# A hybrid attention, convolution, Fourier and expert kernel: the first expert tile's tokens picked by matmuls, weights ahead of casts, attention and preparation cut in units

## The chip, the cores and the metric
The kernel runs on the 8 cores of one Trainium2 chip. Each core computes one item of the batch, and no core talks to another. The metric is the device time of the slowest core in microseconds. Each core has TensorE (PE, matrix multiplication into the 8 banks of PSUM), VectorE (DVE), ScalarE (ACT), GpSimd (POOL) and SyncE (SP). POOL and SP issue the DMAs of this kernel. Each engine executes its instructions in order; semaphores join them.

## The reference
Two layers over 2048 latent tokens and 256 context tokens of width 1024, eight batch items. Cut to what matters:

```
cols = adaln(x) @ w_in                       # 1440 columns for three groups of heads
q = rmsnorm(rmsnorm(cq) @ w_uq); k, v = (rmsnorm(ckv) @ w_ukv), rotary part of k shared
attn = softmax(q k / sqrt(96)) v             # 8 heads, 2048 (+256) queries, 2304 keys
conv = silu(layernorm(depthwise_conv31(a * sigmoid(g))))
four = real(fft2(u)) over positions and channels of a group
x = x + gate * (concat(attn, conv, four) @ w_out)
layer 0: x = x + gate * swiglu(adaln(x))     # inner width 2816
layer 1: x = x + gate * sum over the top 2 of 8 experts of w_e * swiglu_e(adaln(x))
```

Modulation (`ada_w`) gives shift, scale and gate from a vector per batch item. The context goes the same way in layer 0; in layer 1 only its keys and values are used. Weights arrive as fp32; the matmuls are done in bf16. The output is the latent stream.

## The kernel before
**Residual stream.** `xT` (latent) and `cT` (context) hold the stream transposed, fp32, in SBUF for the whole program, as 4 blocks of 512 tokens and one of 256. A line such as `P.mm` records an instruction; the order of the recording is the order on each engine, and waits are derived from what each instruction reads and writes. So everything below has the order in which it is written. Helpers: `mm` L242, `transpose` L247, `act` L269, `tt` L273, `ts` L282, `stt` L296, `copy` L303, `recip` L307, `dma` L321, `gather` L329, `scatter` L336.

**Start.** 18 tiles of x and ctx are read and transposed by PE, with two buffers `xin`. `adab` (ada_w of layer 0, 8 pieces) is allocated in the memory which `xin` had, then `w_in` is loaded (L886).

**Projection.** For each block `adaln_steps` (L501) squares `xT` on ACT, sums over channels by a matmul with ones (`sq,cb`), and writes `hb`; `proj_units` gives 13 units of `w_in` matmuls. The steps for the next block are spread between the units of this one, and end with its last unit.

**Convolution, Fourier.** The convolution is 31 matmuls with diagonal matrices `dg` per 128 channels and block; its layer norm follows each block at once. `ada_rest` loads and multiplies one more piece of ada_w (`adab`) after each block. The Fourier part is matmuls with DFT matrices (`AB`). `out_proj(mixcf)` adds their share of the output projection to `xT` with `stt`.

**Attention.** `prep_steps(h)` makes `qf`, `kf`, `va` and the key scale `rk` of a head. Head 0's are done before attention, the next head's one step for each fourth attention step (`tick`). An attention step is one score matmul (128 keys, 512 queries), an `Exp` on ACT into `pt` and, two steps later (`LA`), the PV matmul. Scores have three PSUM banks. At the end of a query block `recip` and `tt` divide by the sum, from PSUM. `out_proj(mixa)` follows.

**Casts.** The expert weights are read as fp32 and written as bf16 to DRAM (`wsc`, `wsl`) by 48 casts (`mk_cast`, L838) of three DMAs each, on POOL's queue. A cast is an expert and a sixth of its inner width: three matrices, 3.15 MB written, the last sixth half of that. They wait for nothing. One stands before each layer's convolution, 18 lie in each layer's attention, 3 in layer 1's projection; the others are in the FFN and ahead of the experts. `w_outa`, `wr` (FFN weights) and `adab` load through the same queue.

**FFN of layer 0.** Six groups of inner columns (`mk_ffn`), with weights in two buffers `wr`; the first is loaded ahead of `out_proj(mixa)`. SP's queue zeroes the slot buffer `hs` from `zt` (23 DMAs) in that stretch.

**Experts of layer 1** (`moe_layer`, L548). The router transposes `xT` by tiles into token rows, writes x to the output, makes `hrow` (normed rows) and the logits. Slots come from sums by matmul. The 5888 slots are 23 tiles of 256 rows, each tile of one expert. 32 `scatter`s put each row into `hs` at both its slots. Each tile has six chunks of weights `wb[c]`, fetched by `gather` on POOL for the tile's expert; a gather reads `w_all` and so waits for all casts. `prep_h` loads a tile's rows (`hld`), and transposes them by matmuls (`cb,hld`) into `hTt`; `gu` and `down` are the expert matmuls, and a scatter-add puts the result in the output.

## Time and profile before

| | us |
|---|---|
| median of 3 runs | 4246.35 (4244.84 to 4509.96) |
| the profiled execution, device time | 4243.74 |
| its span on the slowest core (core 1) | 4242.7 |
| spans of the 8 cores | 4229.6 to 4242.7 |

| engine | busy us | share | instructions |
|---|---|---|---|
| TensorE matmuls | 3530.8 | 83% | 20731 |
| VectorE | 1568.6 | 37% | 2660 |
| ScalarE | 1579.4 | 37% | 3014 |
| GpSimd | 413.6 | 10% | 442 |

The span runs from the first to the last instruction. A busy share is a mean over stages which have different limits, so a stage must be read by its own rows. The granted clock of TensorE is told as a share of its full 2.4 GHz; its mean is 0.90. The DMA share is the mean busy share of the core's 16 DMA engines. The mean rate of DMA is 99 GB/s over 421.91 MB written; a cast counts with the bytes that it writes.

### The profile page before, as it was taken

What the parts mean: (1) busy time and instruction counts of PE and PEld (TensorE: products, weight loads), DVE (VectorE), ACT (ScalarE), POOL (GpSimd) and SP (SyncE); (2) the same over time, 40 slices, a digit from 0 to 9 for tenths busy, and PEclk for the clock granted to TensorE, in tenths of its full rate; (3) what the DMA queues carried; (4) which work ended last, traced back from release to release, by engine and by line L of the source; (5) the groups of instructions that cost most, each with busy time, mean ns of one, the idle gap of its engine ahead of it and who ended that gap; (6) DMA issues with size and microseconds to landing.
All of it is one profiled execution on the core that took longest, in us unless ns stands there. A gap on an engine that the chain in (4) does not pass through costs nothing.

```text
span 4242.7 us, 60869 instructions; the slowest of 8 cores (4229.6 to 4242.7 us)
## 1 busy us (share of the span) xinstructions
PE 3530.8 (83%) x20731; PEld 1917.3 (45%) x20731; DVE 1568.6 (37%) x2660; ACT 1579.4 (37%) x3014; POOL 413.6 (10%) x442
## 2 busy tenths in 40 slices
PE   4667777777879999767777878838999999999998
PEld 3224322222224555322322222316777777777776
DVE  1333545444544444433444444551222222222222
ACT  2433267777551111243267778321111111111111
POOL 0000201100000000000101010021111111111111
PEclk5778888888989999877888889869999999999999
DMA  7115499992494962633399997161555345425111
GB/s 166 30 26 90 55 108 111 112 106 39 101 162 59 121 93 43 81 38 40 58 108 102 108 102 92 75 228 52 179 200 191 93 131 192 161 56 189 31 26 21
DMA packets 215899, 421.91 MB, mean 99 GB/s; under 512 B 31952, under 2 KB 152272, under 8 KB 207312
## 3 DMA queue, kind: packets, MB, share of 16 engines
q0 software_dynamic: 186432, 347.15, 50.2%
q1 hardware_dynamic: 29168, 70.85, 5.2%
q8 instruction: 177, 2.90, 0.3%
q14 instruction: 122, 1.00, 0.1%
HBM read 833.76 MB, written 192.73 MB: 242 GB/s over the span
## 4 chain that ended last, share of the span: by engine, by line
PE 68%; DVE 10%; ACT 9%; issue 8%; DMA 3%; DVEq 0%; POOL 0%; ACTq 0%; another core or an unknown queue 0%; SPq 0%; POOLq 0%
PE psall L242 68%; DVE rec L307 3%; ACT pt L269 3%; DVE t L296 2%; ACT sqq L269 1%; DVE tmp L296 1%; DMA w_in<-w_in 1%; ACT L269 1%; DMA adab<-ada_w 1%; ACT rs L269 1%; DMA xin<-x 1%; ACT sq L269 1%; PE psall L247 1%; DVE xT L296 1%; DVE kf L282 1%
## 5 line engine op out<-in xcount | busy, mean ns | idle before, releaser
L242 PE MATMUL psall<-hTt,wb 128*128 128x256 bf16 x8096 | 908.5, 273 | 9.0 <-ACT hTt L269 8.6
L242 PEld LDWEIGHTS psall<-hTt,wb 128*128 128x128 bf16 x8096 | 791.5, 98 | 129.3 <-issue 12.7
L269 ACT ACTIVATE pt<-psall,rk 128x512 bf16<-128x512 f32 x1168 | 697.5, 720 | 62.8 <-PE psall L242 58.6
L242 PE MATMUL psall<-pt,va 128*128 128x512 bf16 x1168 | 490.1, 420 | 234.7 <-ACT pt L269 189.0
L273 DVE TENSOR_TENSOR aT<-sg,psall 128x256 bf16<-128x256 f32 x506 | 213.1, 421 | 1020.0 <-PE psall L242 993.1
L269 ACT ACTIVATE sg<-psall 128x256 f32<-128x256 f32 (+1 forms) x524 | 203.9, 390 | 1016.2 <-PE psall L242 1004.4
L242 PE MATMUL psall<-qf,kf 96*128 96x512 bf16 x1168 | 491.7, 422 | 0.0
L242 PE MATMUL psall<-wb,aT 128*128 128x512 bf16 x2024 | 459.2, 379 | 0.0
L242 PEld LDWEIGHTS psall<-pt,va 128*128 128x128 bf16 x1168 | 122.9, 105 | 602.2 <-issue 574.6
L242 PE MATMUL psall<-hT,wr 128*128 128x512 bf16 (+1 forms) x1760 | 354.7, 361 | 11.1 <-ACT hT L269 10.7
L307 DVE RECIPROCAL rec<-psall 64x512 f32<-64x512 f32 (+1 forms) x72 | 228.8, 3177 | 195.7 <-PE psall L242 194.6
L242 PE MATMUL psall<-hb,w_in 128*128 128x512 bf16 (+3 forms) x888 | 245.9, 434 | 58.9 <-ACT hb L269 46.1
L242 PEld LDWEIGHTS psall<-wb,aT 128*128 128x128 bf16 x2024 | 198.0, 98 | 209.6
L242 PEld LDWEIGHTS psall<-hT,wr 128*128 128x128 bf16 x1760 | 172.2, 98 | 185.0 <-issue 21.2
L296 DVE SCALAR_TENSOR_TENSOR xT<-psall,mod,xT 128x512 f32<-128x512 f32 x320 | 235.6, 749 | 46.5 <-PE psall L242 21.2
L269 ACT ACTIVATE sgt<-psall 128x512 f32<-128x512 f32 (+1 forms) x110 | 60.9, 553 | 432.1 <-PE psall L242 421.9
L329 POOL DMA_INDIRECT wb<-wsc,wix x115 | 115.8, 1007 | 931.7 <-PE psall L242 930.3
L242 PE MATMUL psall<-aT,wr 128*128 128x512 bf16 (+1 forms) x880 | 187.3, 365 | 21.1 <-DVE xT L296 19.0
L242 PEld LDWEIGHTS psall<-hb,w_in 128*128 128x128 bf16 (+1 forms) x888 | 100.3, 114 | 182.9 <-issue 118.2
L273 DVE TENSOR_TENSOR aT<-sgt,psall 128x512 bf16<-128x512 f32 (+1 forms) x110 | 69.8, 634 | 288.5 <-PE psall L242 268.0
L242 PEld LDWEIGHTS psall<-qf,kf 96*128 96x128 bf16 x1168 | 121.8, 104 | 71.4 <-issue 40.2
L296 DVE SCALAR_TENSOR_TENSOR t<-psall,vecs,rope 96x512 f32<-96x512 f32 (+3 forms) x144 | 103.2, 717 | 110.7 <-ACT sqq L269 108.1
(227 smaller groups left out, 2995.8 us busy)
## 6 DMA issues: line engine op xcount, KB each, us to landing
wsc<-moe_w_gate POOLq DMA_DIRECT2D x40, 1024.0 KB, 58.8
wsc<-moe_w_up POOLq DMA_DIRECT2D x40, 1024.0 KB, 67.9
wsc<-moe_w_down POOLq DMA_DIRECT2D x40, 1024.0 KB, 76.4
wb<-wsc SPq DMA_DIRECT2D x5, 3072.0 KB, 20.0
adab<-ada_w POOLq DMA_DIRECT2D x8, 1536.0 KB, 14.4
hs<-zt SPq DMA_DIRECT2D x23, 520.0 KB, 23.8
hld<-hs SPq DMA_DIRECT2D x23, 520.0 KB
xin<-x SPq DMA_DIRECT2D x16, 512.0 KB, 3.4
```

Source lines behind the costliest of these rows:

```text
L242: return s.op("pe", lambda: nc.tensor.matmul(out.ap, lhsT=lhsT.ap, rhs=rhs.ap, start=start, stop=stop), reads=[lhsT, rhs], writes=[out])
L247: return s.op("pe", lambda: nc.tensor.transpose(out.ap, in_.ap, ident.ap), reads=[in_, ident], writes=[out])
L269: return s.op("act", lambda: nc.scalar.activation(out=out.ap, in_=in_.ap, func=func, **kw), reads=rd, writes=wr)
L273: return s.op(eng, lambda: e.tensor_tensor(out=out.ap, in0=a.ap, in1=b.ap, op=op), reads=[a, b], writes=[out])
L282: return s.op(eng, lambda: e.tensor_scalar(out=out.ap, in0=a.ap, scalar1=a1, scalar2=None, op0=op0), reads=rd, writes=[out])
L296: return s.op("dve", lambda: nc.vector.scalar_tensor_tensor(out=out.ap, in0=a.ap, scalar=a1, in1=b.ap, op0=op0, op1=op1), reads=rd, writes ...
L307: return s.op("dve", lambda: nc.vector.reciprocal(out=out.ap, in_=in_.ap), reads=[in_], writes=[out])
L329: return s.op("pool", lambda: e.indirect_dma_start(out.ap, None, in_.ap, off, bounds_check=lr, oob_is_err=False), reads=[in_, idx], writes ...
```

## The change
- **Start.** The reads and transposes of x and ctx stand behind the issue of `ada_w` and `w_in`, with four buffers.
- **Norms.** The statistics matmul of a square is recorded one step later, and the next block's `adaln` is done two units earlier.
- **Convolution.** The layer norm of a block follows the next block's convolution (`conv_a`, `conv_b`), the last one the first Fourier part; the cast before the convolution is gone.
- **Head preparation** is cut in units with two PSUM banks of their own. Head 0's run inside `out_proj(mixcf)`, one after each residual update. The key scale's `Ln` and `Exp` are done once a head, and `kf` is squared on DVE.
- **Attention.** A step covers 1024 queries: two score matmuls, one `Exp` over two banks, two PV matmuls; two pairs of score banks. At the end of a query block the result is copied from PSUM to `oe`, and divided in pieces of 128 columns, one small operation per step.
- **Casts.** `w_outa` is loaded ahead of them. One and then 18 are recorded in layer 0's attention, as many in layer 1's; the last one (20 in all there) before the router.
- **Router.** `moe_layer` is a generator: its constants are made in the last head, its 32 half tiles in and after `out_proj(mixa)`. `hrow` is added on POOL. Only `wb[0]` is preloaded early, the others once `xT` is released.
- **Tile 0.** Its first three gathers stand ahead of the scatters, the others behind. `hTt[0]` is the product of `hrow` and one-hot matrices that compare each slot number with the tokens' slots (`m1`, `m2`), 128 matmuls.

The diff, cut:

```diff
@@ adaln_steps
         def stat(dc):
-            P.act(sq[:, dc % 2, 0:n], src[:, dc, t0s:t0s + n], AF.Square)
-            P.mm(ps[:, bk, 0:n], ones(), sq[:, dc % 2, 0:n], dc == 0, dc == 7)
+            if dc < 8:
+                P.act(sq[:, dc % 2, 0:n], src[:, dc, t0s:t0s + n], AF.Square)
+            if dc >= 1:
+                P.mm(ps[:, bk, 0:n], ones(), sq[:, (dc - 1) % 2, 0:n], dc == 1, dc == 8)
...
-        st = [(lambda d=dc: stat(d)) for dc in range(8)] + [rs]
+        st = [(lambda d=dc: stat(d)) for dc in range(9)] + [rs]
         st += [(lambda d=dc: app(d)) for dc in range(8)]
         return st
@@ moe_layer
-        for c in range(2):
-            preload(c)
-        hrow = P.alloc("hrow", [128, 16, HROW], BF16)
+        preload(0)
...
+        def norm_out(tt_, xr):
+            xn = xnr[tt_ % 2]
+            P.stt(xn[:, :], xr[:, :], rst[:, tt_:tt_ + 1], gbc[:, :], ALU.mult, ALU.mult)
+            P.tt(hrow[:, tt_, 0:1024], xn[:, :], sbc[:, :], ALU.add, eng="pool")
+
+        for st_ in range(32):
+            yield
...
+                finish()
+        finish()
+        P.release(xT, gbc, sbc, *xrow, *xnr, junk, *lgT)
+        wb += [P.alloc("wb", [128, 12288], BF16) for _ in range(4)] + [P.alloc("wb", [128, 6144], BF16)]
+        for c in range(1, NCH):
             preload(c)
...
+        for c in range(3):
+            gather(0, c)
         csc = P.chan("scat", bulk=True)
         for tt_ in range(16):
             for k_ in range(2):
                 P.scatter(hs_all, hrow[:, tt_, :].w(lambda a: a.bitcast(U16)), sl[k_][:, tt_:tt_ + 1], csc, order=(tt_ + k_ == 0))
         P.fence("D_hs", 0, NSLOT, csc)
-        for c in range(NCH):
-            gather(0, c)
-        P.release(hrow)
-        yt = [P.alloc("yt", [128, 2, D], F32) for _ in range(2)]
         load_h(0)
         load_h(1)
-        prep_h(0)
+        for c in range(3, NCH):
+            gather(0, c)
+        mbc = P.alloc("mbc", [128, D], F32)
+        bcast(mbc, lambda dc: mod[:, 40 + dc, 0:1])
+        ohs = [P.alloc("ohs", [128, TS], BF16) for _ in range(4)]
+        for tt_ in range(16):
+            o_ = ohs[tt_ % 4]
+            P.ts(o_[:, :], slotc, m1[:, tt_:tt_ + 1], ALU.is_equal)
+            P.stt(o_[:, :], slotc, m2[:, tt_:tt_ + 1], o_[:, :], ALU.is_equal, ALU.add)
+            for dc in range(8):
+                P.mm(ps[:, dc, 0:TS], hrow[:, tt_, dc * 128:(dc + 1) * 128], o_[:, :], tt_ == 0, tt_ == 15)
+        for dc in range(8):
+            P.copy(hTt[0][:, dc, :], ps[:, dc, 0:TS], eng=("act" if dc % 2 else "dve"))
+        P.release(hrow, *ohs)
+        yt = [P.alloc("yt", [128, 2, D], F32) for _ in range(2)]
...
+                if c == 4 and t == 0:
+                    prep_meta(0)
@@ start of layer 0
             w_in_next[0] = w_in_load(0)
+            xin = [P.alloc("xin", [128, D], F32) for _ in range(4)]
+            cx = [P.chan("xin%d" % i_) for i_ in range(4)]
...
+            for n, (src, i, dst, t0) in enumerate(tiles):
+                xb = xin[n % 4]
+                P.dma("sp", xb[:, :], src[i * 128:(i + 1) * 128, :], cx[n % 4])
+                for half in range(2):
+                    bk = (2 * n + half) % 8
...
@@ projection
-                want = len(nxt) * (ui + 1) // len(un)
+                want = min(len(nxt), len(nxt) * (ui + 1) // (len(un) - 2))
@@ convolution
-        cast()
...
+        cjobs = [(yp, goff, b0, n) for (yp, T, goff, blks) in cstreams for (b0, n) in blks]
+        for k in range(len(cjobs)):
+            yp, goff, b0, n = cjobs[k]
+            conv_a(yp, b0, n, k)
+            if k >= 1:
+                conv_b(cjobs[k - 1][1], cjobs[k - 1][2], cjobs[k - 1][3], k - 1)
+            ada_rest()
+        P.release(dg, ypx, ypc)
+        while adk0[0] < 8 and l == 0:
+            ada_rest()
...
         P.release(uT, uTr)
+        conv_b(cjobs[-1][1], cjobs[-1][2], cjobs[-1][3], len(cjobs) - 1)
+        P.release(*[C_[k_] for C_ in cset for k_ in C_], mu, var)
@@ out_proj
-        def out_proj(mixbuf, w_out):
-            for (src, tb0, t0s, n, j) in streams:
...
-                    bk = 1 + m % 6
+                    bk = m % nbk
                     for kk in range(4):
                         P.mm(ps[:, bk, 0:n], w_out[:, kk, m * 128:(m + 1) * 128], mixbuf[:, kk, g0:g0 + n], kk == 0, kk == 3)
                     P.stt(src[:, m, t0s:t0s + n], ps[:, bk, 0:n], mod[:, 16 + m, j:j + 1], src[:, m, t0s:t0s + n], ALU.mult, ALU.add)
+                    if hook is not None:
+                        hook()
@@ preparation of a head
...
+                if hasq:
+                    un += [(qa, None), (qb, None), (ka, None), (va_, None), (qc, qd), (kb, None)]
+                else:
+                    un += [(ka, None), (va_, None), (kb, None)]
+            return un
...
+            def __init__(s_, h, slots):
+                s_.h = h
+                s_.un = prep_units(h)
+                s_.n, s_.slots, s_.k, s_.late = len(s_.un), slots, 0, None
+
+            def unit(s_):
+                if s_.late is not None:
+                    f_, s_.late = s_.late, None
+                    f_()
+                if s_.un:
+                    f_, s_.late = s_.un.pop(0)
+                    f_(6 + unitc[0] % 2)
+                    unitc[0] += 1
 
             def tick(s_):
-                b_ = s_.p1
-                nxt = s_.steps.pop(0) if s_.steps else None
+                s_.k += 1
+                while s_.un and (s_.n - len(s_.un)) * s_.slots < s_.n * s_.k:
...
+        p0 = Prep(0, 1)
+        out_proj(mixcf, w_out, None, 6, p0.unit)
+        P.release(mixcf, w_out)
+        w_outa = P.alloc("w_outa", [128, 4, D], BF16)
+        wload([w_outa[:, :, :]], [w_out_d[l, 0:512, :].rearrange("(k p) c -> p k c", p=128)], "w_outa")
+        cast()
+        p0.flush()
@@ attention
-            qblocks = [(b0, n, list(range(18))) for (b0, n) in XBLK] + ([] if last else [(SEQ, 256, [16, 17])])
+            qblocks = [(0, 1024, list(range(18))), (1024, 1024, list(range(18)))] + ([] if last else [(SEQ, 256, [16, 17])])
...
+        perh = len(its) // NH
+        cstep = (len(its) - 36) // 18
+        cat = set(range(3, 3 + 18 * cstep, cstep))
         for t in range(len(its) + LA):
             if t in cat:
                 cast()
                 h, qi, q0, nq, ki, j, nk = its[t]
...
                     if h + 1 < NH:
-                        pend[h + 1] = Prep(prep_steps(h + 1))
+                        pend[h + 1] = Prep(h + 1, perh - 5)
                     else:
-                        P.release(*[v_ for T in tset for v_ in T.values()])
-                        w_outa = P.alloc("w_outa", [128, 4, D], BF16)
-                        wload([w_outa[:, :, :]], [w_out_d[l, 0:512, :].rearrange("(k p) c -> p k c", p=128)], "w_outa")
-                bs = 2 + (t % 3)
-                P.mm(ps[:, bs, 0:nq], kf[hp][:, j * 128:(j + 1) * 128], qf[hp][:, q0:q0 + nq], True, True)
-                P.act(pt[t % 4][:, 0:nq], ps[:, bs, 0:nq], AF.Exp, scale=rk[hp][:, j:j + 1])
-                if t % 4 == 3 and (h + 1) in pend:
-                    pend[h + 1].tick()
+                        P.release(*[T[k_] for T in tset for k_ in ("sq", "sk", "t1", "t2")])
+                        if last:
...
+                bs = 2 + 2 * (t % 2)
+                nb_ = max(1, nq // 512)
+                for i_ in range(nb_):
+                    w_ = min(512, nq)
+                    P.mm(ps[:, bs + i_, 0:w_], kf[hp][:, j * 128:(j + 1) * 128], qf[hp][:, q0 + i_ * 512:q0 + i_ * 512 + w_], True, True)
+                if nb_ == 2:
+                    P.act(pt[t % 3][:, :].w(lambda a: a.rearrange("p (b c) -> p b c", b=2)), ps[:, bs:bs + 2, :], AF.Exp, scale=rk[hp][:, j:j + 1])
+                else:
+                    P.act(pt[t % 3][:, 0:nq], ps[:, bs, 0:nq], AF.Exp, scale=rk[hp][:, j:j + 1])
+                if (h + 1) in pend:
+                    if t + 3 < len(its) and its[t + 3][0] == h + 1:
+                        pend.pop(h + 1).flush()
+                    else:
+                        pend[h + 1].tick()
             u = t - LA
             if u >= 0:
                 h, qi, q0, nq, ki, j, nk = its[u]
                 hp = h % 2
-                bo = qi % 2
-                P.mm(ps[:, bo, 0:nq], va[hp][:, j, :], pt[u % 4][:, 0:nq], ki == 0, ki == nk - 1)
+                nb_ = max(1, nq // 512)
+                w_ = min(512, nq)
+                for i_ in range(nb_):
+                    P.mm(ps[:, i_, 0:w_], va[hp][:, j, :], pt[u % 3][:, i_ * 512:i_ * 512 + w_], ki == 0, ki == nk - 1)
                 if ki == nk - 1:
...
+                    for i_ in range(nb_):
+                        o_ = oe[oec[0] % 3]
+                        oec[0] += 1
...
+                        for p_ in range(0, w_, 128):
+                            small.append(lambda o_=o_, rc=rc, p_=p_, no=no, do=do:
+                                         P.recip(rc[no:no + 64, p_ % 256:p_ % 256 + 128], o_[do:do + 64, p_:p_ + 128]))
+                            if p_ % 256:
...
@@ last layer
+        if last:
+            cast(len(casts))
+            next(moe)
+            for b in range(4):
+                out_proj(mixa, w_outa, b, 3, (lambda: next(moe)) if b >= 1 else None)
+            P.release(mixa, w_outa)
+            for _ in moe:
+                pass
+            break
         out_proj(mixa, w_outa)
         P.release(mixa, w_outa)
         dump_sb("xTm%d" % l, xT, [128, 8, SEQ])
 
-        if last:
-            cast(len(casts))
-            moe_layer()
-            break
 
```

## Where instructions stand

TensorE in layer 0's attention, before, in the first head (`pt` is the exponential, `va` values, `qf` and `kf` queries and keys, `cqn` the normed latent that the next head is prepared from, `sqq` its square):

```order
L242 MATMUL psall<-pt_135,va_116 128x512 [waits s_act]
L242 MATMUL psall<-qf_112,kf_114 128x512
L242 MATMUL psall<-pt_132,va_116 128x512 [waits s_act]
L242 MATMUL psall<-qf_112,kf_114 128x512
L242 MATMUL psall<-cqn_70,wq_107 96x512 [waits s_dve]
L242 MATMUL psall<-cqn_70,wq_107 96x512 x2
L242 MATMUL psall<-cqn_70,wqr_108 96x512 x3
L242 MATMUL psall<-cb_47,sqq_126 128x1 x4
L242 MATMUL psall<-pt_133,va_116 128x512 [waits s_act]
L242 MATMUL psall<-qf_112,kf_114 128x512
```

and in the change:

```order
L244 MATMUL psall<-cqn_72,wq_110 96x512 [waits s_act]
L244 MATMUL psall<-cqn_72,wq_110 96x512 x2
L244 MATMUL psall<-pt_135,va_118 128x512 x2
L244 MATMUL psall<-qf_114,kf_116 128x512 [waits s_act]
L244 MATMUL psall<-qf_114,kf_116 128x512
L244 MATMUL psall<-cqn_72,wqr_111 96x512 [waits s_dve]
L244 MATMUL psall<-cqn_72,wqr_111 96x512 x2
L244 MATMUL psall<-pt_133,va_118 128x512 x2
L244 MATMUL psall<-qf_114,kf_116 128x512 [waits s_act]
L244 MATMUL psall<-qf_114,kf_116 128x512
```

A step now has two PV and two score matmuls; the wait for ScalarE stands at the score matmul, and a preparation unit between steps is three matmuls where it was ten.

GpSimd's queue where experts start, before (`sl` slots, `wix` weight rows; `c_cast` the casts' semaphores, `c_wp` a preload's):

```order
L336 DMA hs<-hrow_235,sl_267 5888x1040
L336 DMA hs<-hrow_235,sl_268 5888x1040
L329 DMA wb_233<-wsc,wix_274 128x12288 [waits c_cast1,c_cast5,c_cast4,c_cast6,c_cast7,c_cast3,c_cast0,c_cast2,s_dve,c_wp0]
L329 DMA wb_234<-wsc,wix_274 128x12288 [waits s_dve,c_wp1]
L329 DMA wb_245<-wsc,wix_274 128x12288 [waits c_wp2,s_dve]
```

and in the change:

```order
L275 TENSOR_TENSOR hrow_235<-xnr_240,sbc_229 128x1024 [waits s_dve]
L331 DMA wb_234<-wsc,wix_276 128x12288 [waits c_cast5,c_cast0,c_cast2,c_cast1,c_cast7,c_cast6,c_cast3,c_cast4,c_wp0,s_dve]
L331 DMA wb_246<-wsc,wix_276 128x12288 [waits c_wp1,s_dve]
L331 DMA wb_247<-wsc,wix_276 128x12288 [waits c_wp2,s_dve]
L338 DMA hs<-hrow_235,sl_269 5888x1040 [waits c_zero]
L338 DMA hs<-hrow_235,sl_270 5888x1040
```

The first gather, with its wait for all eight cast channels, stood behind the last scatter and now stands ahead of the first one, behind the adds that make `hrow`.

## Rows read from the trace of the kernel before

**Rows 1.** The page's part 4, the chain that ended last: shares by engine.

```profile
PE 68%; DVE 10%; ACT 9%; issue 8%; DMA 3%; DVEq 0%; POOL 0%; ACTq 0%; another core or an unknown queue 0%; SPq 0%; POOLq 0%
```

**Rows 2.** Timeline of PE at the boundaries: start us, length us, operation [idle before <-releaser].

```profile
111.98 3.62 PE L242 MATMUL psall<-hb,w_in 128*96 128x512 bf16 x8 [12.47 <-DMA w_in<-w_in]
...
501.44 0.62 PE L242 MATMUL psall<-ckvn,wkn 128*64 128x512 bf16 x2
...
1119.81 0.38 PE L242 MATMUL psall<-pt,va 128*128 128x512 bf16 x1
...
1168.51 0.58 PE L242 MATMUL psall<-hT,wr 128*128 128x512 bf16 x1 [3.46 <-ACT hT L269]
...
1755.68 0.59 PE L242 MATMUL psall<-sq,cb 128*128 128x512 bf16 x2
...
2110.05 0.62 PE L242 MATMUL psall<-ckvn,wkn 128*64 128x512 bf16 x2
...
2874.88 1.86 PE L242 MATMUL psall<-cb,hld 128*128 128x128 bf16 x16 [54.80 <-DMA hld<-hs]
...
2930.49 0.72 PE L242 MATMUL psall<-cb,hld 128*128 128x128 bf16 x10
```

**Rows 3.** Timeline of POOL: first cast of the first and the last burst, layer 0's attention.

```profile
502.31 1.13 POOL L321 DMA_DIRECT2D wsc<-moe_w_gate  x1
...
958.40 0.88 POOL L321 DMA_DIRECT2D wsc<-moe_w_gate  x1 [141.01 <-issue]
```

**Rows 4.** DMA queues, 500 to 1000 us: packets, MB, share of 16 engines.

```profile
q0 software_dynamic: 46176, 51.91, 95.6%
```

**Rows 5.** Windows: length, busy (x) of PE, PEld, DVE, ACT, POOL, PEclk, DMA share, GB/s.

```profile
10.00:60.00 50.00, 31.88 (x136) 26.10 (x136) 11.76 (x17) 11.04 (x18) 0.00 (x0) 0.60 0.59 189
70.00:110.00 40.00, 8.21 (x123) 4.25 (x120) 6.34 (x12) 11.58 (x17) 1.32 (x7) 0.50 1.05 162
111.98:330.97 218.99, 150.32 (x721) 64.22 (x721) 72.50 (x123) 89.76 (x151) 2.12 (x4) 0.76 0.12 23
2690.00:2700.00 10.00, 9.86 (x47) 4.25 (x46) 8.46 (x12) 0.00 (x0) 0.00 (x0) 1.00 0.99 388
```

**Rows 6.** Timeline of PE, layer 1's last head: two score matmuls of following steps.

```profile
2677.49 0.38 PE L242 MATMUL psall<-qf,kf 96*128 96x512 bf16 x1
...
2678.07 0.38 PE L242 MATMUL psall<-qf,kf 96*128 96x512 bf16 x1
```

**Rows 7.** Waits of PE, 501.44 to 1119.8: total us, times, longest us.

```profile
PE psall L242 <- ACT pt L269: 94.6, 54, 4.1
```

**Rows 8.** Waits of PE, 111.98 to 330.97, layer 0's projection.

```profile
PE psall L242 <- ACT sq L269: 41.7, 24, 3.4
PE psall L242 <- ACT hb L269: 18.8, 8, 3.7
```

**Rows 9.** Waits of PE, 330.97 to 501.44.

```profile
PE psall L242 <- DMA adab<-ada_w: 18.8, 1, 18.8
PE psall L242 <- DVE ybf L303: 10.3, 6, 4.5
```

**Rows 10.** Groups by shape, whole span: line, engine, operation xcount | busy, mean ns | idle before.

```profile
L296 DVE SCALAR_TENSOR_TENSOR xT<-psall,mod,xT 128x512 f32<-128x512 f32 x320 | 235.6, 749 | 46.5 <-PE psall L242 21.2
L269 ACT ACTIVATE sq<-xT 128x512 bf16<-128x512 f32 x96 | 57.1, 621 | 82.4 <-PE psall L242 74.3 <-DVE xT L296 7.3
L273 DVE TENSOR_TENSOR hrow<-xnr,sbc 128x1024 bf16<-128x1024 f32 x16 | 19.6, 1226 | 1.7
L269 ACT ACTIVATE sq<-cT 128x256 bf16<-128x256 f32 x24 | 9.3, 408 | 1.9 <-PE psall L242 1.9
```

**Rows 11.** The page's part 6, DMA issues: KB each, median us from issue to landing.

```profile
hs<-zt SPq DMA_DIRECT2D x23, 520.0 KB, 23.8
```

**Rows 12.** Waits of PE, 1755.68 to 1976.14, layer 1's projection.

```profile
PE psall L242 <- ACT sq L269: 43.4, 27, 3.4
```

**Rows 13.** Timeline of POOL: the last of 32 scatters; all take as long.

```profile
2863.92 0.96 POOL L336 DMA_INDIRECT hs<-hrow,sl  x1 [0.27 <-issue]
```

346 lines of the change are left out of this document (169 added, 177 removed).

## The prediction

> **What bounds the kernel now.** I read the chain of waits first. TensorE is 68% of it and DMA 3% [rows 1]: in most stages its order, and what it waits for, set the end, and hardly a transfer. Then I took the stages' boundaries from TensorE's timeline [rows 2]: layer 0 reaches its first head at 501.4 us, ends attention at 1119.8 and begins the dense FFN at 1168.5; layer 1 starts at 1755.7 and reaches its first head at 2110.1. The first hT of expert tile 1 is made at 2930.5 [rows 2]. Each piece between can be forecast by itself.
>
> The third view is GpSimd's queue and its transfers. The casts of the expert weights go out in bursts, the first at 502.3, the last at 958.4 [rows 3]. From 500 to 1000 us the queue is busy 95.6%, for 51.91 MB [rows 4]: these are 18 casts, and 95.6% of 500 us and a slow end put them between 502.3 and some 988. That is 106.9 GB/s. So the 618 us of attention in layer 0 hide 486 us of casts, with 130 to spare. Attention that is shorter than its casts meets a wall.
>
> Within attention, where nothing else is to do, a step of 512 queries comes each 0.58 us [rows 6]. Over the stage TensorE waits 94.6 us for exponentials [rows 7], and besides for the ends of the softmax, which read PSUM.
>
> **Start to layer 0's first head.** x is now read behind ada_w and w_in. From 10 to 60 the DMA share is 0.59, from 70 to 110 it is 1.05 [rows 5], so some 20 us of a resource that bounds the start lie unused; the first projection waits 12.5 us for w_in [rows 2]. I take -25 (the ends: -10, if only that wait goes; -45, if the loads filled all of 10 to 60 and the x tiles hid behind).
> Projection: TensorE waits 41.7 us for squares and 18.8 for hb [rows 8], 60 in sum. With the statistics a step late and the next block ready two units early these go, but for some 10 in the first block. The clock is 0.76 in this stage, with TensorE busy for 150 us [rows 5]; at 0.87 that is 131, 18 less. -68.
> Convolution: the 18.8 us for adab, whose load stands behind a cast that is now gone, 10.3 for ybf [rows 9] and some 2 of LN: -31. DFT -4, from the rows for AB.
> Output projection with head 0's prep in its gaps: 40 residual updates of 0.749 us on VectorE are 30 us [rows 10], and about as many VectorE operations of prep, of 0.6 us, come between: 54 instead of 39, and 5 of waiting for w_uq. +20. The separate prep (501.4 to 535) is inside the next piece and goes.
> 501.4 - 25 - 68 - 31 - 4 + 20 = **393**.
>
> **From there to the FFN: the casts.** w_outa now goes first on the queue (1.05 MB at 106.9 GB/s: 10 us), then 19 casts of 55.05 MB: 515 us. wr0, the FFN's first weights, stands behind them on the same queue: 3.15 MB, 29 us. SP's zeroing DMAs (23 of 520 KB: 12 MB [rows 11]) take engines from these: 37 us at most, since both transfers fit between 1121 and 1168.5 now. 10 + 515 + 29 + 37 = **591**, where 667 stand now.
> TensorE needs less. For the Exp of 1024 elements the rows of a square give the slope: 512 take 0.621 us and 256 take 0.408 [rows 10], so 512 more cost 0.43, and a step 0.58 + 0.43 = 1.01, against twice 0.58. The other end is a step in which nothing overlaps (below). A head has 36 steps, and the next head's 30 prep units add 10 to 17 us: 47 to 54 us, 8 heads 420, and 46 for output projection and adaLN, 466 in all. The casts decide, 125 us later: attention saves 150 to 200 us, and the stage 76.
>
> **FFN** of layer 0: 587 - 10 = **577**, by waits for statistics like those of [rows 8].
> **Layer 1 to its first head**, 354.4 us now: projection waits 43.4 us for squares [rows 12] and has the same form; the first block's own statistics, some 15 us, lie inside this piece, so less goes than in layer 0: -55. Convolution -5, DFT -8, output projection with prep +18: **304**.
>
> **From layer 1's first head to the end.** w_outa 10, 20 casts of 56.6 MB 529, wb[0] 10; the x rows to the output (8.4 MB) 26 and wb[1..5] (four of 3.15 MB and a half) 44, at 320 to 390 GB/s as at 2690 [rows 5]: 619 us until the first gather may start, for each gather of tile 0 waits for all eight cast channels. Computation would be there sooner: attention 400, output projection with the router 37, its rest 30, the slots 50, in all 517; and GpSimd, which is in order and issues casts until +470, may hold its hrow adds back to 536. VectorE takes 1.226 us for such an add now [rows 10]; GpSimd has no row, so I bound it by 1.2 and 4.8 us, the time between two router tiles, and neither end reaches the wall.
> A rule speaks against this move. The Trainium skill has an add on GpSimd at 1.96 times VectorE's time (GPSIMD Engine Reference, Elementwise), an estimate of 2.4 us here, and lets an operation of VectorE that reads two SBUF inputs block while GpSimd reads SBUF (SBUF — State Buffer, Who interferes with whom). By it VectorE would lose up to 16 x 2.4 = 38 us: 574, still short of 619, and no row here shows it.
> Tile 0's three gathers stand ahead of the 32 scatters on GpSimd, so the scatters begin at +623 and end 39 us later (32 x 1.23 [rows 13]). Now TensorE waits 54.8 us there for hld [rows 2]; with tile 0 picked by one-hot matmuls this goes; these 128, of 256 columns and under 0.3 us each, lie under the wait for the wall. First expert matmul at +625, three chunks to +656, then a wait for a gather issued behind the scatters, +667, and 21 us to the prep of tile 1: +688. From there as now, 4242.7 - 2930.5 = 1312. **2000**, against 2133 now.
>
> **Sum**: 393 + 591 + 577 + 304 + 2000 = **3865 us**, against a span of 4242.7 and the profiled execution's 4243.7; the median of the runs is 4246, so I say 3868.
>
> **Rivals.**
> *No cast wall* (0.13). The casts speed up once the loads before them are gone. For it: the hardware queue reached 388 GB/s [rows 5]. Against it: 95.6% busy in 500 us [rows 4]. The second piece is 466, the last 400 + 37 + 30 + 50 + 51 + 1312 = 1880: 3620 (3660 by the skill's rule above).
> *A wide step of 1.9 us* (0.13), where PV waits are not covered by two score buffers. Second piece 304 x 1.9 + 46 = 624, last one 547 + 168 + 1312 = 2027: 3925. For it: the 94.6 us of now [rows 7]. Against it: 0.58 with three buffers [rows 6].
> *Smaller savings* (0.17). Loads that collide with x, VectorE full in both output projections, squares that still come late: 25 to 30 us in each of three places: 3950.
> *The one-hot tile does not do what it says* (0.05). Its gathers wait for the casts and then land behind scatters: the first expert matmul comes no sooner than now after the slots, +42: 3910.
> *Slower than before* (0.02): score, Exp and PV in series, since with two score buffers a matmul waits for the Exp two steps back. At the low clock a matmul takes 0.45 (8 in 3.62 us [rows 2]), the wide Exp 0.62 + 0.43 [rows 10]: 4 x 0.45 + 1.05 = 2.85 us. Second piece 304 x 2.85 + 46 = 912, last one 821 + 168 + 1312 = 2301: 4487. It decides from 2.6 us a step. Against it: the matmuls of the next step don't depend on this Exp.
> My forecast's own case has 0.50.
>
> **Chances.** Two per cent is about what a measurement of this kernel can tell from no change. All cases but the last end far under 4160: faster 0.95, same 0.03 (mishaps that add up), slower 0.02. The range, 3690 to 3980, takes in the smaller savings and the wide step, and reaches halfway to no wall.
>
> **What would show it.** GpSimd's queue over 90% busy from 395 to 985, and TensorE idle for some 100 us on a DMA before the first hT,wr; the first w_in matmul near 87; projections of 150 and 165 us; in layer 1 a wait for wb before the first hTt,wb, with the scatters behind it; wide steps at 1.0 to 1.1 us, bound by ScalarE. If the FFN starts right after mixa's output projection, the wall is wrong; if the clock stays at 0.76 in the projection, its term is.

## The result and the profile after

The changed kernel takes 4010.8 us in the median of four executions (3960.2 to 4228.6). In two of the four the cores of one die ran at a lower clock; the ratio leaves these out. It is **0.935 of before, 95% interval 0.926 to 0.943**: 6.5% faster, where 8.9% was forecast. The profiled execution took 3960.2 us and its span is 3959.1; all stages below are read there, on core 1 where no core is named. The forecast was 3868. Its range (3690 to 3980) holds the other two executions (3960 and 3977) and not the median.

By stage, us of the span, from TensorE's first or last matmul of a kind:

| piece | before | forecast | after | miss |
|---|---|---|---|---|
| first w_in matmul | 112.0 | -25 | 99.5 (-12.5) | +12.5 |
| projection, layer 0 | 219.0 | -68 | 182.4 (-36.6) | +31 |
| convolution and Fourier | 131.3 | -35 | 107.3 (-24.0) | +11 |
| output projection of these, with head 0 | 39.2 | +20 | 54.3 (+15.1) | -5 |
| from there to the FFN | 667.0 | 591 | 587.2 | -4 |
| FFN | 587.2 | 577 | 578.2 | +1 |
| layer 1 to its first head | 354.4 | 304 | 339.7 | +36 |
| from there to the end | 2132.6 | 2000 | 2010.5 | +10.5 |

The misses add up to 94 us, the difference of 3959 and 3865, and 86 of them lie ahead of each layer's attention.

The chain that ended last, part 4 of the page, after (before: [rows 1]):

```profile
PE 68%; DVE 9%; ACT 8%; issue 6%; another core or an unknown queue 6%; DMA 3%; DVEq 0%; POOL 0%; ACTq 0%; SPq 0%; POOLq 0%
```

New is 6% that the chain puts down to a queue it does not know. These are 97 us ahead of the FFN, 77 ahead of the first gather and 45 in the first expert tile, the three places of which the experiments treat (the chain in order of time: start us, length us):

```profile
933.28 97.07 another core or an unknown queue
2468.60 77.20 another core or an unknown queue
2555.11 7.79 another core or an unknown queue
2563.14 37.67 another core or an unknown queue
```

TensorE's boundaries after, which answer [rows 2]:

```profile
99.48 0.63 PE L244 MATMUL psall<-hb,w_in 128*96 128x512 bf16 x1 [4.61 <-ACT hb L271]
...
447.30 0.60 PE L244 MATMUL psall<-pt,va 128*128 128x512 bf16 x2
...
888.20 1.01 PE L244 MATMUL psall<-mixa,w_outa 128*128 128x512 bf16 x3 [2.34 <-DVE oe L305]
...
1030.71 0.58 PE L244 MATMUL psall<-hT,wr 128*128 128x512 bf16 x1 [97.42 <-DMA wr<-ffn_w_down]
...
1608.89 0.59 PE L244 MATMUL psall<-sq,cb 128*128 128x512 bf16 x2
...
2549.45 9.54 PE L244 MATMUL psall<-hTt,wb 128*128 128x256 bf16 x64 [34.17 <-DMA wb<-wsc,wix]
...
2643.47 1.06 PE L244 MATMUL psall<-cb,hld 128*128 128x128 bf16 x16
```

The wall (the next stage's weights stand behind the casts in one queue) is where it was forecast: TensorE waits 97.4 us for wr0 and 34.2 for the first gather. GpSimd's queue (packets, MB, share of 16 engines) from 445 to 975, against [rows 4]:

```profile
q0 software_dynamic: 48455, 54.73, 95.5%
```

Its timeline, with the loads of wr0 (the FFN's first weights) as the next thing behind the last cast, 508 us after the first:

```profile
444.97 0.91 POOL L323 DMA_DIRECT2D wsc<-moe_w_gate  x1
...
952.28 0.75 POOL L323 DMA_DIRECT2D wsc<-moe_w_down  x1
953.01 0.92 POOL L323 DMA_DIRECT2D wr<-ffn_w_gate  x1
```

### The profile page after: what moved, and what is told of

It reads as the page before. It is cut to its first block, busy times and chain, and to the rows that moved or that the text cites. A ratio compares the mean times of both kernels' runs of the same rounds, so it can differ in the third digit from the quotient of the medians.

```text
span 3959.1 us, 59552 instructions; the slowest of 8 cores (3902.7 to 3959.1 us)
## 1 busy us (share of the span) xinstructions
PE 3356.9 (85%) x20843; PEld 1919.2 (48%) x20843; DVE 1642.1 (41%) x3100; ACT 1438.5 (36%) x2214; POOL 451.1 (11%) x458
## 4 chain that ended last, share of the span: by engine, by line
PE 68%; DVE 9%; ACT 8%; issue 6%; another core or an unknown queue 6%; DMA 3%; DVEq 0%; POOL 0%; ACTq 0%; SPq 0%; POOLq 0%
PE psall L244 68%; ACT pt L271 2%; DVE rec L309 2%; DMA xin<-x 2%; DMA out<-xrow 1%; ACT L271 1%; DVE xT L298 1%; DVE tmp L298 1%; DVE oe L305 1%; DVE t L298 1%; ACT sq L271 1%; DVE kf L305 1%; ACT hb L271 1%; ACT sqq L271 0%
## 5 line engine op out<-in xcount | busy, mean ns | idle before, releaser
L244 PE MATMUL psall<-hTt,wb 128*128 128x256 bf16 x8096 | 913.3, 274 | 81.1 <-DMA wb<-wsc,wix 34.2
L271 ACT ACTIVATE pt<-psall,rk 128x1024 bf16<-128x1024 f32 (+1 forms) x592 | 619.6, 1092 | 123.4 <-PE psall L244 122.1
L244 PE MATMUL psall<-hT,wr 128*128 128x512 bf16 (+1 forms) x1760 | 353.1, 360 | 102.5 <-DMA wr<-ffn_w_down 97.4
L244 PE MATMUL psall<-pt,va 128*128 128x512 bf16 x1168 | 361.7, 387 | 51.7 <-DVE oe L305 51.1
L244 PE MATMUL psall<-qf,kf 96*128 96x512 bf16 x1168 | 358.1, 387 | 16.5 <-ACT pt L271 12.2
L309 DVE RECIPROCAL rec<-oe 64x128 f32<-64x128 f32 x272 | 252.2, 938 | 10.0
L244 PE MATMUL psall<-hb,w_in 128*128 128x512 bf16 (+3 forms) x888 | 225.0, 411 | 30.2 <-ACT hb L271 13.6
L244 PEld LDWEIGHTS psall<-qf,kf 96*128 96x128 bf16 x1168 | 104.8, 99 | 195.1 <-issue 113.9
L244 PEld LDWEIGHTS psall<-pt,va 128*128 128x128 bf16 x1168 | 99.1, 98 | 170.3 <-issue 101.2
L244 PEld LDWEIGHTS psall<-aT,wr 128*128 128x128 bf16 x880 | 82.8, 98 | 117.7 <-issue 40.0
```

The costliest lines, as they stand in the source:

```text
L244: return s.op("pe", lambda: nc.tensor.matmul(out.ap, lhsT=lhsT.ap, rhs=rhs.ap, start=start, stop=stop), reads=[lhsT, rhs], writes=[out])
L271: return s.op("act", lambda: nc.scalar.activation(out=out.ap, in_=in_.ap, func=func, **kw), reads=rd, writes=wr)
L309: return s.op("dve", lambda: nc.vector.reciprocal(out=out.ap, in_=in_.ap), reads=[in_], writes=[out])
```

## The experiments

Each edit is made in the changed kernel. "Tile 0" is the time from the first expert matmul to the first hT of tile 1. "After a layer's first head" counts from the end of the output projection ahead of that layer's attention. The eight cores lie on two dies, cores 0 to 3 and 4 to 7.

**1. four_casts_to_ffn**

```diff
-        cstep = (len(its) - 36) // 18
+        ncat = 18 - (0 if last else 4)
+        cstep = (len(its) - 36) // ncat
...
-                        cast(2 if jobn <= 1 else 1)
+                        cast({0: 3, 1: 3, 2: 2, 3: 2}.get(jobn, 0))
```

> Four of the 18 casts in layer 0's attention are recorded in the FFN instead (3, 3, 2, 2 in its first groups); all else as in the changed kernel. Theory of the wall: TensorE's 97.4 us of waiting for wr0 are due to the casts ahead of it on the same queue, 29.4 us each, so four fewer (118 us) remove the wait: the FFN begins 90 to 97 us earlier (from 587 us after the end of the first output projection to 490 to 497), and the kernel takes 3865 to 3875 in the profiled execution, against 3960; if the FFN's own loads now come late, up to 20 of it come back there. Rival, that wr0 is late because the DMA engines are full of other transfers whatever their order: the wait shrinks by less than half, 3910 or more.

Measured: the FFN began at 936.5, 94 us earlier, without a wait for wr0:

```profile
936.50 1.03 PE L244 MATMUL psall<-hT,wr 128*128 128x512 bf16 x2 [3.53 <-ACT hT L271]
```

The wall is shown. But the kernel took 3930 in the median and 3941 in the profiled execution (ratio 0.926, 0.924 to 0.928), and not 3870: the FFN grew from 578 to 615 us (26.1 of it a wait for adab, which is in the same queue), and layer 1's first gather came 612 to 642 us after its first head instead of 597 to 607. The places to which I moved casts were not free.

**2. exp_in_halves**

```diff
-                    P.act(pt[t % 3][:, :]..., ps[:, bs:bs + 2, :], AF.Exp, ...)
+                    for i_ in range(2):
+                        P.act(pt[t % 3][:, i_ * 512:i_ * 512 + 512], ps[:, bs + i_, :], AF.Exp, ...)
```

> Each Exp over 1024 columns is two of 512, all else as in the changed kernel. A step's ScalarE time goes from 1.09 to about 1.44 us. Theory of the wall: layer 0's attention takes 441 + 304 x 0.3 = some 530 us instead of 441, but the casts end no later, so the FFN begins within 10 us of where it did, and TensorE's wait for wr0 shrinks from 97 to about 10. In layer 1 attention is some 85 us longer, of which the 34 us wait for the first gather and some more are cover: +45 to +60. In all 4005 to 4025 in the profiled execution. Rival, that attention's speed decides in both layers: +175, 4135. Second rival, that ScalarE has room in a step and TensorE decides: no change at all, 3960, and a step of 1.2 us as before.

Measured: attention 447.4 in layer 0 instead of 440.9, 428 instead of 408 in layer 1, and 3976 in all (3972 in the profiled execution; 0.937, 0.935 to 0.940), which is what the change itself takes (14). My theory was wrong, since I had costed the extra time on top of a step. The second rival holds: ScalarE had room. The groups of the Exp in layer 0, whole and in halves (xcount | busy us, mean ns | idle before):

```profile
L271 ACT ACTIVATE pt<-psall,rk 128x1024 bf16<-128x1024 f32 x285 | 304.2, 1109 | 73.2 <-PE psall L244 72.6
```

```profile
L271 ACT ACTIVATE pt<-psall,rk 128x512 bf16<-128x512 f32 x572 | 343.3, 722 | 43.2 <-PE psall L244 42.8
```

The wide Exp takes 1.11 us and two narrow ones 1.44, and layer 0's attention gets 7 us of these 0.33 a step (20 in layer 1). The width of the instruction is not what made attention short. The step of 1024 queries with its pairs of score banks stays in this experiment and was not tested by itself.

**3. softmax_end_from_psum**

```diff
-                        P.copy(o_[:, 0:w_], ps[:, i_, 0:w_])
...
-                        for p_ in range(0, w_, 128):
-                            small.append(...)          # pieces of 128 columns, one a step
...
+                        P.recip(rc[no:no + 64, 0:w_], ps[do:do + 64, i_, 0:w_])
+                        P.tt(mixa[...], ps[no:no + 64, i_, 0:w_], rc[no:no + 64, 0:w_], ALU.mult)
```

> The end of a query block is again as before the change: reciprocal and multiplication read PSUM, 512 columns at once, with no copy to oe and no pieces of 128 columns; the wide steps stay. Read on attention (first PV to first matmul with mixa): 588 us before the change in layer 0 (536.8 to 1124.7) and 441 with it (447.3 to 888.2), 541 and 408 in layer 1; halving the Exp cost only 7 and 20. Theory: PV banks are now the same two for each query block, so the next block's PV waits for two reciprocals of 3.4 us and two multiplications of 0.7, 8 us, 16 times a layer less what is covered: attention 520 to 570 in layer 0, so that this edit, and not the wide Exp, made most of the gain. Rival: with preparation in small units VectorE has the room, and attention stays under 480; then the units made the gain.

Measured: 557.8 us in layer 0, as the theory said, and 534.2 in layer 1, against 440.9 and 408.3; 588 and 541 were those before the change. The kernel took 4053 in its one execution. TensorE's waits in layer 0's attention (total us, times, longest):

```profile
PE psall L244 <- DVE mixa L275: 117.1, 31, 5.3
```

Before the change TensorE's waits in this stage were the 94.6 us for exponentials of [rows 7] and these, and with the change the two below:

```profile
PE psall L242 <- DVE mixa L273: 45.3, 8, 5.9
```

```profile
PE psall L244 <- DVE oe L305: 29.9, 24, 2.5
PE psall L244 <- ACT pt L271: 9.0, 19, 0.7
```

Attention got 147 us shorter by the change in layer 0 and 133 in layer 1. Of these, 117 and 126 are lost again without the copy and its pieces. But this does not say that the end of the softmax had cost 117 before. There TensorE waited 45.3 us for it and 94.6 for exponentials. The wide step puts each query block's PV into the same two banks, and it is this step that needs the copy: without it the waits for mixa rise to 117.1, with it those for exponentials stay at 9.0. What the copy does and what the pieces do was not told apart. The wall takes up most of the 117: with this edit the FFN began at 1049.9, 19 us later than with the change.

**4. gathers_behind_scatters**

```diff
-        for c in range(3):
-            gather(0, c)
         csc = P.chan("scat", bulk=True)
...
-        for c in range(3, NCH):
+        for c in range(NCH):
             gather(0, c)
```

> All six gathers of tile 0 stand behind the 32 scatters, as they did before the change; the one-hot matmuls stay. In the changed kernel the scatters run from 2550.9 to 2590.6, and in that time TensorE stands still for 4.7, 17.8 and 16.3 us in the first expert matmuls, once for nothing that the profile shows and else for a ScalarE that waits for another queue. Theory A: these stalls come from the scatters (instructions that the engines fetch by DMA are late behind them). Behind the slots, at about 2490, the scatters would run under TensorE's wait for the casts, end at about 2530, and the first expert matmul comes at 2549 as before, now without stalls: the first hT of tile 1 is 38 to 43 us earlier, 3917 to 3922. Theory B: the stalls belong to the first pass through the expert code (tables, first use): no change, 3955 to 3965. Theory C, my prediction's: the fourth gather behind the scatters held tile 0 back: 10 us earlier.

The two executions that the ratio counts took 3976 and 3997 (0.939, 0.934 to 0.944): no gain. The trace is read on core 5. Scatters were the first thing in GpSimd's queue and stopped after six:

```profile
2497.41 0.97 POOL L338 DMA_INDIRECT hs<-hrow,sl  x1 [0.27 <-issue]
2547.22 0.97 POOL L338 DMA_INDIRECT hs<-hrow,sl  x1 [48.83 <-issue]
```

All theories had overlooked this: casts and scatters share one queue, so scatters can't run under the wait for casts. The first gather came 641 to 650 us after layer 1's first head (597 to 607 with the change), and tile 0, beside which no scatter ran now, took 51 to 60 us.

**5. tile0_from_rows**

```diff
-        ohs = [...]        # and 128 one-hot matmuls
+        P.release(hrow)
+        prep_h(0)
```

> Tile 0's hT is made from the rows that scatters wrote and a DMA read back, as before the change, and not by one-hot matmuls; gathers stand where the change has them. The first expert matmul then waits for the scatters, the load of hld and the transposes: 2590.6 + 5 + 4 = about 2600 instead of 2549. Theory A (scatters stall the engines anyway): in the changed kernel tile 0 has got only 13 us of its work done by 2601, so one-hot matmuls are worth 5 to 15 us: 3965 to 3975. Theory of the prediction (tile 0's first three chunks run under the scatters): worth 42 us: about 4002.

Measured: 3983 (0.938, 0.936 to 0.940), 7 us over the change in 14. The first hT of tile 1 comes some 710 us after layer 1's first head (695 to 714), where the change has 695 to 701 on the cores of one die and 668 to 673 on those of the other. So the one-hot matmuls are worth some 15 us on the first and some 40 on the second, and the slower die ends last. Two different things hold tile 0 up. On the slower die TensorE stops and goes on again, here on core 1, behind the 64 matmuls of the row at 2549.45 above (time, busy us, then the wait before it in brackets):

```profile
2563.73 1.87 PE L244 MATMUL psall<-hTt,wb 128*128 128x256 bf16 x8 [4.74 <-ACT sg L271]
2583.35 1.87 PE L244 MATMUL psall<-hTt,wb 128*128 128x256 bf16 x8 [17.75 <-issue]
2601.48 7.39 PE L244 MATMUL psall<-hTt,wb 128*128 128x256 bf16 x48 [16.26 <-ACT sg L271]
```

On the other die there is no such stop. There tile 0 has a single wait, of 14 to 15 us on each of the four cores, ahead of the fourth chunk, for the gather that stands behind the 32 scatters; core 4:

```profile
2588.43 10.04 PE L244 MATMUL psall<-hTt,wb 128*128 128x256 bf16 x64 [15.35 <-DMA wb<-wsc,wix]
```

**6. half_the_scatters**

```diff
-            for k_ in range(2):
+            for k_ in range(1):
                 P.scatter(
```

> Of the 32 scatters of token rows to expert slots only the 16 for the first expert of each token are done; the rows of second experts stay zero. All else as in the changed kernel. From the first expert matmul to the first hT of tile 1 it took 91.7 to 94.3 us on the cores of one die and 66.6 to 68.2 on the other, where 49.1 us is what it takes with no scatter running. Theory: each scatter holds up the instruction streams of the core, so the excess of 43 and 18 us halves: 68 to 73 and 56 to 60 us. Rival: the excess is the time in which the engines first run this code, whatever the number of scatters: 92 and 67.

Measured, tile 0 on the eight cores, from the first expert matmul and the first cb,hld matmul behind it in each core's timeline:

```
core                  0     1     2     3     4     5     6     7
change (again)      91.7  94.3  91.9  93.5  68.2  66.6  67.3  67.2
all 32 (9)          68.5  66.0  68.4  66.4  93.6  94.4  92.4  96.2
half the scatters   51.6  51.5  51.3  51.6  71.1  72.4  76.2  76.1
spread_casts        49.1  49.1  49.1  49.1  49.1  49.1  50.0  49.9
```

Which die is the slower one differs between chips. The second row is experiment 9, which has all 32 scatters and ran on the chip of the third; there the second die is the slower one. On it the excess over 49 falls from some 45 us to 22 to 27. Half the scatters, half the excess, and none where the scatters are over before tile 0 begins (cores 0 to 3 of the last row): so the scatters cause the stops. That they delay the engines' instructions fits the idle time that no engine explains, and is not shown.

On the faster die the excess falls from 17 to 19 us to 2, but for another reason. The fourth gather is issued 21 to 22 us after the first expert matmul instead of 41 to 43, and the wait for it is gone. That scatters stop the engines there is not seen anywhere. In spread_casts they ran beside the one-hot matmuls. On core 0 these stood still, while the 128 of core 4, on the other die, went through beside the scatters:

```profile
2428.30 1.86 PE L244 MATMUL psall<-ohs,hrow 128*128 128x256 bf16 x8 [5.88 <-issue]
2442.38 1.86 PE L244 MATMUL psall<-ohs,hrow 128*128 128x256 bf16 x8 [12.21 <-issue]
2455.03 7.26 PE L244 MATMUL psall<-ohs,hrow 128*128 128x256 bf16 x48 [10.79 <-DVE ohs L298]
```

```profile
2392.69 15.74 PE L244 MATMUL psall<-ohs,hrow 128*128 128x256 bf16 x128 [0.71 <-DVE ohs L298]
```

**7. old_statistics**

```diff
-            if dc >= 1:
-                P.mm(ps[:, bk, 0:n], ones(), sq[:, (dc - 1) % 2, 0:n], dc == 1, dc == 8)
+            P.mm(ps[:, bk, 0:n], ones(), sq[:, dc % 2, 0:n], dc == 0, dc == 7)
...
-                want = min(len(nxt), len(nxt) * (ui + 1) // (len(un) - 2))
+                want = len(nxt) * (ui + 1) // len(un)
```

> Only the two edits on the norms are undone: the statistics matmul stands in the step of its square again, and the next block's norm ends with the last unit. Read on the projection of each layer (first w_in matmul to first convolution matmul), which took 219.0 and 210.9 us before the change and 182.4 and 174.8 with it. Theory: all of the 36 us are these two edits, since nothing else in the stage changed, so it takes 215 to 220 and 207 to 212 us. Rival: part of it is the cleared GpSimd queue (one more adab load on time) or the clock after a denser start; then it stays under 205.

Measured: 220.2 and 218.1 us, against 182.4 and 174.8; before the change it was 219.0 and 210.9. The whole of the 36 us is these two edits; in layer 1 the stage is even 7 us longer than before.

**8. units_by_weight**

```diff
-            un = [kr_a, lambda: lat(1, 0), lambda: lat(1, 1), kr_b, lambda: latn(1)]
+            un = [(kr_a, 8), (lambda: lat(1, 0), 8), (lambda: lat(1, 1), 8), (kr_b, 0)]
...
+            un += [(lambda: four(0), 8), (kr_c, 0), (lambda: latn(1), 0), (lambda: lat(0, 0), 8), ...
...
-                want = min(len(nxt), len(nxt) * (ui + 1) // (len(un) - 2))
+                want = min(len(nxt), len(nxt) * cw // max(tw, 1))
```

> In the projection the steps of the next block's norm are given out in proportion to the matmuls of a unit, not one share per unit, and the sums for the key's rotary part stand one unit later than the multiplication that writes the same bank (the first Fourier unit between them). The changed kernel's projection still waits 18.7 us for squares, 12.6 for sg on VectorE and 5 for sg on ScalarE. Theory: the squares are late in the units that hold one to four small matmuls and still get a share of steps, and sg is the bank's release; so both go: the projection takes 160 to 168 us instead of 182.4, and 152 to 160 instead of 174.8. Rival: ScalarE (92 us busy) and VectorE (77) are in each other's way and the waits only move: within 5 us of 182.4.

Measured: 159.2 and 151.4 us, just under the theory, but for half of its reason. TensorE's waits in layer 0's projection, first in the changed kernel, then here:

```profile
PE psall L244 <- ACT sq L271: 18.7, 11, 3.0
PE psall L244 <- DVE sg L275: 12.6, 5, 2.7
PE psall L244 <- ACT hb L271: 7.0, 6, 4.6
PE psall L244 <- ACT sg L271: 5.3, 4, 1.5
```

```profile
PE psall L244 <- ACT sq L271: 21.1, 18, 2.0
PE psall L244 <- ACT hb L271: 11.9, 15, 4.6
...
PE psall L244 <- DVE sg L275: 1.2, 1, 1.2
```

The waits for the bank (sg) went, those for squares did not.

**9. statistics_two_late**

```diff
-                P.act(sq[:, dc % 2, 0:n], src[:, dc, t0s:t0s + n], AF.Square)
-            if dc >= 1:
+                P.act(hout[:, dc, ho:ho + n], src[:, dc, t0s:t0s + n], AF.Square)
+            if dc >= 2:
```

> The changed kernel with the norm's squares written to eight places (the block of hb or hT that the norm will fill later) instead of two, and each statistics matmul two steps behind its square instead of one. In the changed kernel TensorE waits 18.7 us for squares in layer 0's projection, 21.1 in layer 1's. Theory: a square is still being made when its matmul comes, one step later, in the units with few matmuls; with two steps it is not: the wait falls under 8 us and the projection is 10 to 15 us shorter, 168 to 172 instead of 182.4 and 160 to 165 instead of 174.8. Rival: the square itself starts late, since ScalarE is behind with other work of the block (93 us busy of 182, in the same order): the wait moves to another square or to hb, and the stage stays within 4 us.

Measured: 164.7 us in layer 0's projection, 17.7 less, more than the theory's 10 to 15, and no wait for squares is left among the view's rows. From 99 us on the longest is now this one:

```profile
PE psall L244 <- DVE sg L275: 11.5, 5, 2.6
```

**10. last_ln_before_fourier**

```diff
+        conv_b(cjobs[-1][1], cjobs[-1][2], cjobs[-1][3], len(cjobs) - 1)
         sc_x = 1.0 / np.sqrt(SEQ * 64.0)
```

> The layer norm of the last convolution block stands ahead of the Fourier matmuls, not behind their first part. The Fourier stage (first cb,uT matmul to the first matmul of the output projection) took 30.0 and 31.3 us before the change, 41.0 and 42.0 with it. Theory: the norm's five VectorE operations now stand ahead of a copy to mixcf on which TensorE waits (7.0 us), and the clock is low for the 16 matmuls behind that gap; so the stage goes back to 30 to 33 us, and the convolution is longer by 2. Rival: what makes it longer is the output projection's preparation (weights for queries and keys) on VectorE and GpSimd: the stage stays above 38.

Measured: the Fourier stage 34.9 us instead of 41.0, the convolution 72.5 instead of 66.4: nothing in sum (107.5 and 107.3), and 97.4 against 100.0 in layer 1. The norm costs its 6 us in either place. Of the 11 us that Fourier lost, 5 stay unexplained.

**11. x_in_two_parts**

```diff
+            read_tiles(0, 12, 4)
...
         for f in mk_adaln(0):
             f()
+        if l == 0:
+            read_tiles(12, 18, 2)
```

> At the start only 12 of the 18 x and ctx tiles are read and transposed ahead of the first block's norm, the other 6 behind it; the loads of adab2 follow those. In the changed kernel x tiles come 4.4 us apart, with the DMA share at 1.03, the last is transposed at 86, and only then the first block's norm (13 us) leads to the first w_in matmul at 99.5. Theory: my term for the start (-25, measured -12.5) forgot that norm, which stood behind x once x comes last; with it ahead of the last 6 tiles the first w_in matmul comes at 85 to 90. Rival: the DMA, whatever the order, brings w_in and x only by then and TensorE waits for w_in instead: 95 to 100.

Measured: first w_in matmul at 102.2, the projection 177.3 instead of 182.4. The theory was wrong. The size is near the rival's 95 to 100, but its reason does not hold either: no wait for w_in stood there. What bounds the start is open.

**12. spread_casts**

```diff
+        if last:
+            cast(2)          # ahead of the convolution
...
+        if not last:
+            cast()           # behind the last ada_w load
...
+        cast(2)              # ahead of out_proj(mixcf)
         p0 = Prep(0, 1)
...
-        cast()
...
+        ncat = 16
```

> The same 48 casts, but spread over stretches in which the DMA queues are nearly idle: in layer 0 one behind the last ada_w load and two ahead of the output projection of conv and Fourier, 16 in attention (19 in the change); in layer 1 two at the convolution, two ahead of that output projection, 16 in attention (20). Theory of the wall: 29.4 us per cast. Layer 0's FFN begins 3 x 29 = 80 to 88 us earlier after the first output projection's end, at about 500 us instead of 586; the FFN keeps its 578. In layer 1 the casts end some 118 us earlier, and the first gather is bound by the slots, at about 555 us after that projection's end instead of 600: -45. In all 3825 to 3845 in the profiled execution. Rival: w_uq, w_ukv and w_outa, behind casts in the queue, come late and give back more than 30: 3870 or more.

Measured: **3826 us, 0.901 (0.898 to 0.905)**, in the range of the theory. The FFN begins 491 to 497 us after the first output projection (561 to 587 with the change) and takes 577 to 584 (577 to 581). In layer 1 the first expert matmul comes 591 to 600 us after the first head on the cores of one die, where the one-hot matmuls stopped beside the scatters, and 549 to 555 on those of the other; tile 1 comes at 640 to 649 instead of 695 to 701, and at 598 to 604 instead of 668 to 673.

**13. all_together** (8, 11 and 12 in one)

> The spread casts, the projection's units by weight and x in two parts together. By stage against the changed kernel: start -12, projection -23 and -23, wait for wr0 -90, layer 1's wall -40: the profiled execution 3825 - 12 - 46 = 3767 if no wall comes back; since compute is 35 us shorter from the first cast to the FFN only in that the casts start earlier with it, nothing of it is lost: 3760 to 3785. Rival: the casts again bound a piece (GpSimd's queue is busy from 380 to 880), and half of the projection's 46 is lost: 3790 to 3805.

Measured: 3799 (0.895, 0.893 to 0.896), the rival's number and its reason. The projections were 151.8 and 151.1, but TensorE waited for wr0 again:

```profile
PE psall L244 <- DMA wr<-ffn_w_down: 35.4, 1, 35.4
```

**14. after_again**, the base of that call

> The changed kernel itself, on the same chip as the others of this call, as their base: 3955 to 3975 in undisturbed runs. The first expert matmuls stand still for some 40 us while the scatters run on the cores of one die, some 15 on the other, as before.

Measured: 3976 (0.936, 0.935 to 0.938).

**15. all_but_x** (8 and 12, and on top of them)

```diff
-        ncat = 16
+        ncat = 16 if last else 15
...
-                        cast(2 if jobn <= 1 else 1)
+                        cast(2 if jobn <= 2 else 1)
```

> Spread casts and the projection's units by weight, with x read as in the changed kernel, and one more cast of layer 0 taken from attention to the FFN (15 in attention, 7 in the FFN). With everything together, TensorE still waited 35.4 us for wr0. Theory of the wall: a cast is 29.4 us, and x in two parts brought nothing, so the wait falls to 0 to 8 and the FFN, with one more cast, is longer by at most 6: 3762 to 3778 in the profiled execution against 3795 with everything together. Rival: what is gained before the FFN is waited for in layer 1, as the first gather then comes when the casts end: 3785 to 3795.

Measured: ratio 0.891 (0.889 to 0.892), and 3778 to 3785 us in the four executions that it counts, a few us above the theory and below the rival. On cores 0 to 3 of the profile no wait for wr0 is left.

**16. last_version** (9 and 15 in one)

> Spread casts (15 in layer 0's attention, 7 in the FFN, 16 in layer 1's attention), the projection's units by weight, and the norm's squares in eight places with their matmuls two steps late. Theory, by stage: projections 156.5 - 17 = 140 and 151 - 16 = 135, all else as with the spread casts and seven casts in the FFN (3777 to 3785 in undisturbed runs): 3740 to 3755. Rival: with 140 us the projection is at what TensorE needs, the waits for hb and the clock take the gain, or the casts bound layer 1 again: 3765 or more.

Measured: **3737 us in the median, ratio 0.879 (0.877 to 0.881)**, just under the theory. Layer 0's projection took 139 to 147 us on the eight cores, layer 1's 132 to 134. The stops beside the scatters are still there: the first expert matmul comes 591 to 613 us after layer 1's first head on one die and 556 to 562 on the other. This version beats both kernels: 12.1% under before, against 6.5 for the change.

## Why the prediction was wrong in size

**The failed step is "Projection", in both layers: -68 and -55 forecast, -36.6 and -36 measured.** It is 50 of the 94 us (31 in layer 0, 19 in layer 1's piece). The mechanism was right: undoing the two edits gives all of it back (7). The term was mis-sized. It had 50 us of waits that "go" and 18 of a higher clock; in layer 0 TensorE's idle time in the stage fell by 25.5 us (68.7 to 43.2) and its busy time by 11.1 (150.3 to 139.2). I had taken all but 10 of the 60 us of [rows 8] for waits that vanish. One step of lateness left 18.7 us of waits for squares. And when TensorE no longer stood still for the next block's norm, the block's own waits grew: for sg on VectorE from 6.6 (a row of the view of [rows 8] that is not shown) to 12.6, for sg on ScalarE to 5.3. Experiments 8 and 9 took away 23 and 17.7 us, and the last version, with both, stands at 139 to 147: the forecast 151 was within reach of the stage, but not with this change. The granted clock did rise as I had assumed, 0.76 to 0.82 [rows 5], by half of what I took; the window of after (columns as there), layer 0's projection:

```profile
99.50:281.90 182.40, 139.18 (x721) 63.25 (x721) 77.24 (x129) 93.25 (x158) 2.12 (x4) 0.82 0.13 24
```

**Convolution and Fourier**: -24 for -35, and in layer 1 +4 for -13. The convolution gave what was forecast (101.3 to 66.4). What I had at -4 and -8, Fourier, became +11 twice. I had moved a norm to a place and costed it at nothing, without naming what VectorE does next there: a copy to mixcf, for which TensorE then waits 4.9 us in layer 0 and 7.0 in layer 1. Experiment 10 shows 6 of the 11 and that moving it back gains nothing.

**Start**: -12.5 for -25. The unused DMA time was found and filled (share 1.03 from 10 to 70), but x is then late, the first of its tiles 4.4 us apart where they were 2.8, and the 13 us of modulation and norm of the first block stand behind the last of them. Experiment 11 did not get it back.

**The casts' wall** was right, in place and size: 587.2 for 591 (561 to 587 on the eight cores), a wait of 97.4 for "some 100", 601 for 625 in layer 1. Attention itself took 441 for 420 and was hidden, as said. My account of its gain was half right. The waits for exponentials went from 94.6 to 9.0, but the wide Exp instruction has 7 us of the gain, and without another end of the softmax most of it would be gone (3); I had that wait only as a half sentence. And the gain is not of waits alone, as the windows before and after show: of 147 us, TensorE's busy time gave 66, at a granted clock of 0.95 for 0.87.

```profile
536.80:1124.70 587.90, 445.36 (x1875) 150.90 (x1876) 277.97 (x310) 432.24 (x801) 33.76 (x41) 0.87 0.77 85
```

```profile
447.30:888.20 440.90, 379.81 (x1864) 149.72 (x1864) 317.44 (x523) 359.97 (x420) 42.18 (x52) 0.95 0.99 107
```

**Tile 0**: on the slowest core the first matmul to tile 1 took 94 us where I had 63, and it began 24 earlier than I had it; that the sum held is luck. The wait that I had charged, 11 us for the fourth gather, is what the cores of the other die show, with 14 to 15. On the slower die, which sets the time, the stops beside the scatters came instead, and I had no term for them. My rival "does not do what it says" (+42) had their size and not the reason.

**GpSimd's adds** took 2.35 us, 1.92 times VectorE's 1.23 [rows 10]. The Trainium skill has 1.96 (GPSIMD Engine Reference, Elementwise), and the trace agrees nearly. The wait of VectorE is seen too, and costs less than the 38 us I derived. Beside an add, the VectorE operation with two SBUF inputs (xnr) takes up to 2.40 us instead of 1.28, and the residual updates (xT), with one input in PSUM, keep their 0.70. The Trainium skill says the same (SBUF — State Buffer, Who interferes with whom): two SBUF inputs contend with GpSimd's reads, one does not. VectorE, then two of the adds:

```profile
2391.28 1.28 DVE L298 SCALAR_TENSOR_TENSOR xnr<-xrow,rst,gbc 128x1024 f32<-128x1024 f32 x1 [0.73 <-ACT rst L271]
2392.48 1.40 DVE L298 SCALAR_TENSOR_TENSOR xT<-psall,mod,xT 128x512 f32<-128x512 f32 x2
2394.17 2.04 DVE L298 SCALAR_TENSOR_TENSOR xnr<-xrow,rst,gbc 128x1024 f32<-128x1024 f32 x1 [0.29 <-ACT rst L271]
2396.14 1.40 DVE L298 SCALAR_TENSOR_TENSOR xT<-psall,mod,xT 128x512 f32<-128x512 f32 x2
2397.46 2.40 DVE L298 SCALAR_TENSOR_TENSOR xnr<-xrow,rst,gbc 128x1024 f32<-128x1024 f32 x1
```

```profile
2392.77 2.36 POOL L275 TENSOR_TENSOR hrow<-xnr,sbc 128x1024 bf16<-128x1024 f32 x1 [32.41 <-DVE xnr L298]
2396.42 2.35 POOL L275 TENSOR_TENSOR hrow<-xnr,sbc 128x1024 bf16<-128x1024 f32 x1 [1.29 <-DVE xnr L298]
```

In the mean of the 16, xnr takes 1.61 us, where it took 1.28 before the change: 16 x 0.33 = 5 us in all.

## What to carry to other kernels

A background transfer that was hidden sets the end as soon as the work above it gets shorter; count its bytes against the new stage, and spread it over stretches with an idle queue, not behind what another stage loads through the same queue. A wait in the profile is not all gain: when it goes, take half until you have named the next thing that the engine waits for. And a gain with several edits in one stage should be costed by edit: here the wide instruction, which looked like the point, was worth 7 us in layer 0, and the wide step would have lost 117 us again if PSUM had not been freed early. Last, read a stage on more than the slowest core: in tile 0 the two dies lose time for two different reasons.

## What the hardware showed unexpectedly

While 32 scatters of token rows ran (2551 to 2590 on core 1), TensorE, ScalarE and VectorE stopped and went on several times on the cores of one die, and tile 0 took some 43 us more there; 16 scatters cost 22 to 27. On the cores of the other die the same scatters stopped nothing that a trace shows. Why the dies differ is open. And a DMA on GpSimd's queue may have to wait long to be issued at all while casts fill that queue: the seventh scatter waited 49 us (4).
